# One fp32r product with high and low parts in place of a plain fp32 one, in the first attention of a two-block layer kernel

## What is computed

```
log_f = log_sigmoid(proj[..., COL_F:COL_RX] + b_forget)
c = cumsum(log_f, axis=1)
logits = einsum('bhqd,bhkd->bhqk', qb, kh) * scale
logits = logits + cb[..., :, None] - c[:, :, None, :]
probs = softmax(where(causal, logits, -inf))
```

## Time and profile before

| | before |
|---|---|
| median of 3 runs | 2224.82 us |
| lowest and highest | 2224.47, 2226.2 us |
| span of the profiled execution | 2226.0 us |
| its own total time | not given apart from the span; the slowest of the three runs has 2226.2 us |
| TensorE busy | 2156.0 us, 97% |
| DVE, ACT busy | 1316.3 us, 59%; 900.9 us, 40% |
| mean granted clock of TensorE | 0.997 |

### The profile page before, as it was taken

One profiled execution on the slowest core, in us unless ns is written; L12 is line 12 of the kernel. 1 busy time (PEld: TensorE's weight loads), 2 busy tenths in 40 slices (PEclk: granted clock), 3 DMA queues, 4 the chain that ended last, 5 costly groups with the idle time before them and its releaser, 6 DMA issues.

```text
span 2226.0 us, 31963 instructions
## 1 busy us (share of the span) xinstructions
PE 2156.0 (97%) x12035; PEld 1698.3 (76%) x12035; DVE 1316.3 (59%) x1788; ACT 900.9 (40%) x1188; POOL 15.7 (1%) x30
## 2 busy tenths in 40 slices
PE   9999999999889888999999999999999999999998
PEld 8887888655445444888888888888888888888886
DVE  7798566432222223766667665777777777764453
ACT  4564455411111112554435454554434343433342
POOL 1000000000000000000000000000000000000000
PEclk9999999999999999999999999999999999999999
DMA  7765466899999998556654555546666665666664
GB/s 252 214 204 152 133 186 207 319 421 420 420 422 421 421 421 336 178 173 218 211 173 162 162 157 185 169 152 190 189 188 188 188 188 188 188 209 191 196 191 131
DMA packets 283328, 518.39 MB, mean 233 GB/s; under 512 B 22048, under 2 KB 194128, under 8 KB 258512
## 3 DMA queue, kind: packets, MB, share of 16 engines
q1 hardware_dynamic: 280416, 505.50, 66.2%
q0 software_dynamic: 2800, 11.34, 1.5%
HBM read 514.63 MB, written 5.27 MB: 234 GB/s over the span
## 4 chain that ended last, share of the span: by engine, by line
PE 81%; DMA 11%; DVE 5%; ACT 2%; issue 1%; SPq 0%; DVEq 0%; ACTq 0%
PE acc L717 29%; PE acc L738 25%; PE acc L741 12%; DMA mw<-in_w_expert_up 7%; PE ps L1162 5%; PE acc L1242 3%; DMA mw<-in_w_expert_gate 2%; DVE wlo L1973 2%; DMA mw_late<-in_w_expert_up 2%; PE tp L826 1%; PE ps L894 1%; PE tp L1120 1%; PE tp L1110 0%; PE tp L909 0%; PE ps L841 0%
## 5 line engine op out<-in xcount | busy, mean ns | idle before, releaser
L1973 DVE TENSOR_TENSOR wlo<-raw,whi 128x1024 fp32r<-128x1024 f32 x572 | 675.9, 1220 | 209.5 <-ACT whi L1460 205.3
L738 PE MATMUL acc<-xhl,whi 128*128 128x512 f32 x2496 | 790.6, 398 | 1.6 <-DVE wlo L1973 0.7
L1460 ACT ACTIVATE whi<-raw 128x1024 fp32r<-128x1024 f32 x572 | 582.0, 1054 | 350.1 <-DMA raw<-in_w_down 132.1
L741 PEld LDWEIGHTS acc<-xhl,wlo 128*128 128x128 f32 x2496 | 468.9, 188 | 110.8
L741 PE MATMUL acc<-xhl,wlo 128*128 128x256 f32 x2496 | 490.8, 278 | 0.0
L738 PEld LDWEIGHTS acc<-xhl,whi 128*128 128x128 f32 x2496 | 381.4, 189 | 5.8 <-issue 3.0
L1162 PE MATMUL ps<-mw,xg_turn 128*64 128x256 f32 x1536 | 177.2, 384 | 29.3 <-DMA mw<-in_w_expert_gate 22.6
L1162 PEld LDWEIGHTS ps<-mw,xg_turn 128*64 128x64 f32 x1536 | 111.3, 138 | 98.7 <-issue 27.9
L717 PE MATMUL acc<-whi,xhl 128*128 128x512 f32 x480 | 155.9, 395 | 0.0
L717 PE MATMUL acc<-whi,ah 128*128 128x512 f32 x336 | 130.7, 389 | 0.0
L717 PE MATMUL acc<-wlo,ah 128*128 128x512 f32 x336 | 130.7, 389 | 0.0
(11 more groups left out here) (457 smaller groups left out, 2394.9 us busy)
## 6 DMA issues: line engine op xcount, KB each, us to landing
raw<-in_w_in SPq DMA_DIRECT2D x352, 256.0 KB, 3.0
raw<-in_w_up SPq DMA_DIRECT2D x352, 256.0 KB, 2.9
mw<-in_w_expert_up SPq DMA_DIRECT2D x52, 1024.0 KB, 16.5
mw<-in_w_expert_gate SPq DMA_DIRECT2D x50, 1024.0 KB, 17.4
mw<-in_w_expert_down SPq DMA_DIRECT2D x48, 1024.0 KB, 17.7
raw<-in_w_down SPq DMA_DIRECT2D x176, 256.0 KB, 3.3
raw<-in_w_out SPq DMA_DIRECT2D x128, 256.0 KB, 3.1
raw<-in_w_ple_gate SPq DMA_DIRECT2D x64, 256.0 KB, 3.3
```

The costliest lines, as they stand in the source:

```text
L738: pe.matmul(out(ct).rearrange("p (m n) -> p m n", m=2), wh[:, ct * P:ct * P + P], ahl[:, :, k, :], start=first, stop=False, skip_group_che ...
L741: mm = pe.matmul(out(ct)[:, S:2 * S], wl[:, ct * P:ct * P + P], ahl[:, 0, k, :], start=False, stop=last, skip_group_check=True)
L1460: act.activation(whi[:, m % RING, :], raw[:, m % RING, :], ACT.Copy).then_inc(hi_ready, 1)
L1973: dve.tensor_tensor(wlo[:, m % RING, :], raw[:, m % RING, :], whi[:, m % RING, :], ALU.subtract).then_inc(lo_ready, 1)
```

## The change

A second, fp32r, copy of negsel is made by ACT in two pieces: rows 0 to 31 of negsel go to partitions 0 to 31 and to 32 to 63 of negsel_r. DVE sets c_hl to zero, rounds c_cum to fp32r into partitions 0 to 7 of it, and writes the remainder to partitions 32 to 39. TensorE then multiplies the 64 partitions at once, so high and low part are subtracted in one fp32r product. The memset of c_cum is left out. The attention waits for ACT's copies (neg_ready) and no longer for late_in, for which ACT has waited by then. negsel_r lies where w_ing was, c_hl where diag is in other stages.

```diff
+        negsel_r = at("negsel_r", 77, [P, HEADS1, P], F32R)
+        c_hl = at("c_hl", 91.5, [P, S], F32R)
...
+        neg_ready = sem("neg_ready")
...
             pe.wait_ge(c_ready, 1)
-            pe.wait_ge(late_in, 48)
+            pe.wait_ge(neg_ready, 2)
 
             def minus_c(u, o, w):
 
-                return pe.matmul(o, negsel[:, u, :], c_cum[:, 0:w], start=False, stop=True, skip_group_check=True)
+                return pe.matmul(o, negsel_r[0:64, u, :], c_hl[0:64, 0:w], start=False, stop=True, skip_group_check=True)
...
             consume(4)
             root(3)
             squares(3)
+            for part in (0, 32):
+                act.activation(negsel_r[part:part + 32, :, :], negsel[0:32, :, :], ACT.Copy).then_inc(neg_ready, 1)
 
             consume(4)
             act.wait_ge(f_abs, 1)
...
-            own(dve.memset(c_cum[:, :], 0.0))
...
             dve.wait_ge(f_y, 1)
             own(dve.memset(z_1[:, :], 1.0))
+            own(dve.memset(c_hl[:, :].bitcast(F32), 0.0))
             log1p(z_y[:, :], z_z[:, :], z_q[:, :], z_s[:, :], z_n[:, :])
             own(dve.scalar_tensor_tensor(z_f[:, :], z_f[:, :], 0.0, z_n[:, :], ALU.min, ALU.subtract))
             mine()
-            dve.tensor_tensor_scan(c_cum[0:8, :], z_1[:, :], z_f[:, :], 0.0, ALU.mult, ALU.add).then_inc(c_ready, 1)
+            own(dve.tensor_tensor_scan(c_cum[0:8, :], z_1[:, :], z_f[:, :], 0.0, ALU.mult, ALU.add))
+            mine()
+            own(dve.tensor_copy(c_hl[0:8, :], c_cum[0:8, :]))
+            mine()
+            dve.tensor_tensor(c_hl[32:40, :], c_cum[0:8, :], c_hl[0:8, :], ALU.subtract).then_inc(c_ready, 1)
             dve.wait_ge(ms_root, 1)
             dve.reciprocal(inv[:, :], inv[:, :]).then_inc(inv_ready, 1)
```

## The result

The changed kernel takes 2236.43 us (median of 5, 2235.61 to 2239.2) against 2224.82 us (median of 5, 2224.47 to 2227.52): a ratio of 1.0049, 95% interval 1.0038 to 1.006, so 11.6 us more, where 5.65 were forecast. The time lies above the range. The profiled execution has a span of 2237.3 us (its own total is 2239.13) against 2226.0. A span is 1.8 to 1.9 us shorter than the total of its execution wherever both are given, so the profile before belongs to an execution of some 2227.9 us (an estimate from that difference), and both profiles are of slower executions of their kernels.

What follows compares the result with a forecast made beforehand. TensorE, 81% of the chain, was taken as the bound, with DVE's row setting the value projection stage. 2.97 - 0.25 + 1.53 + 1.4 = +5.65 us on 2224.82 gives 2230.5 us, range 2224.5 to 2232.5.

Steps and rivals of the forecast that it cites:

- TensorE's wait at 191: Value projection stage: TensorE waits 2.8 us at 191.41 for inv_lo, delayed by ACT's and DVE's added work.
- fall of the clock: After TensorE's stall near 191 us the granted clock drops to 1.2 GHz: +1.4 us (1.3 to 1.7).
- attention: Attention, 217 to 284 us: faster fp32r matmuls against tile-height changes, +1.53 us in sum over eight units (-3.9 to about +3.8).
- the fp32r rate: Attention's score matmuls: fp32r instead of plain fp32 saves 0.42 to 0.48 us a unit, 3.4 to 3.9 in eight.
- 27 borders: Attention: switches between 128-row and 64-row products, 0.2 us each, 12 on the path in units 0 to 2, 15 in the others.
- a unit led by TensorE: Attention units 0 to 2, TensorE without a gap: four borders count, +0.31 us each, 0.93 in three.
- a unit led by DVE: Attention units 3 to 7, DVE's chain the bound: three borders count, +0.12 us each, 0.6 in five.
- What is late at 284 us stays late.: From the attention's end to the kernel's end: the delay carries through unchanged, expert weight loads shifting too; nothing added.
- Rival 1: Value projection and attention: borders and stall, but no fall of the clock; +4.25, 2229.1 us; chance 0.28.
- Rival 2: Attention: borders cost nothing at L1022 in all eight units; -0.7, 2224.1 us (2225.5 with the clock's fall); chance 0.20.
- Rival 3: Attention: 128-column fp32r matmuls stay at 0.22 us; +1.3 more, 2231.8 us; chance 0.05.
- Rival 4: After 191.4 us: the stall is absorbed, replacing waits further on; +1.3, 2226 us; chance 0.03.

Runs made afterwards that it cites:

- 128 rows: Changed kernel with the product over 128 rows, ACT's copies later, DVE's c_hl operations moved into its q/k loop, four tiny fp32 products added in the first run-in: 2222.74 us, 0.9988.
- 64 rows: Changed kernel, still 64 rows, with ACT's copies later, DVE's c_hl operations moved into its q/k loop, four tiny fp32 products added in the first run-in: ratio 1.0008.
- the stall alone: Changed kernel with ACT's copies and DVE's operations kept, but TensorE multiplying plain fp32 negsel and c_cum, c_cum's memset back: 2231.79 us, ratio 1.0024.
- the best kernel without padding: Changed kernel with 128 rows, later ACT copies and moved DVE operations, without the four added fp32 products (16 instructions) in the first run-in: 2228.85 us, ratio 1.0011.
- the kernel before with padding: Kernel before the change plus four plain fp32 products of 4 columns (16 instructions) in the first run-in, nothing else: 2227.66 us, ratio 1.0009.

## Why the prediction was wrong

Point by point, forecast and trace:

| step | forecast, us | shown, us |
|---|---|---|
| ACT's copies | +1.94 | 2.14 (first split 169.30 to 171.44) |
| DVE's operations | +1.03 | 1.13 (16.17 less 15.04) |
| TensorE's wait at 191 | 2.8 | 2.89 |
| fall of the clock | +1.4 | with the wait +4.31 at 217 us, so 1.3 to 1.4 |
| removed memset | -0.25 | -0.28 at the first matmul |
| attention | +1.53 | +1.42 (to the output projection), +1.54 (first to last product) |
| of it the fp32r rate | -3.4 to -3.9 | -3.4 (128 rows: -0.85 at 217 us, -4.28 at 284) |
| of it 27 borders | +5.4 | +4.85 (64 rows: -0.93, +0.49) |
| a unit led by TensorE | +0.31 | +0.29 to the end of the fill's first two matmuls, +0.30 from unit to unit |
| a unit led by DVE | +0.12 | +0.10 |
| to the end | 0 | +6.1 |

**The step that failed is "What is late at 284 us stays late."** The forecast put the term from there to the end at nothing, and the runs showed 6.1 us. The sentence held for DMA and semaphores, which it argued from: +5.15 us at 284 are +5.22 at 850.89. What it left out is that the change also makes TensorE's program shorter, and that a program is itself fetched. The row that would have asked for it stood in the trace of the kernel before: a wait of 3.9 us on "issue", right behind a branch, can be an engine that waits for its own instructions. None of the four rivals had it. With 6.1 us more the forecast would have been 2236.6 us, against 2236.43; that they agree to 0.2 us is partly luck, since the sum up to 284 us was 0.5 too high and the kernel's own runs lie up to 3.6 us apart.

The forecast also took the profile before for an execution as long as the slowest of the three (2226.0 beside 2226.2), and so set a span beside totals; it used only the difference, so nothing in its sum changes. Its clock term is 1.7 less 0.4, which is 1.3 and not 1.4, inside its own bounds.

The sum up to 284 us, +5.65, came out at +5.15. A part of the difference is at the start: TensorE was 0.58 us ahead at 165 us and not 0.25. But this place scatters: the twelve other kernels lie between -0.02 and -1.57 us there, the unchanged program part included, as the clock rises sooner or later behind the first matmuls (the first 32 matmul records take 6.58 us in some executions and 5.31 in another).

Rival 1 (no fall of the clock) did not happen; in all seven kernels that stood still for 2.5 us or more there (2.53 to 3.26) the clock fell, for 3.4 or 6.8 us, and in none of the others. The forecast had one length of the fall; it has two, and the longer costs 1.5 us more (the stall alone: 5.8 instead of 4.3). Its reason, that the stall is longer than the two waits it knew, isn't borne out as a rule: behind the same wait of 2.06 us at 420 us of the kernel before, the clock fell in nine traces and not in the five others, and of the six in which TensorE stood still for 2.3 to 2.7 us at 613 it fell in one. So the fall was forecast rightly, and in part by luck. Rival 2, borders that cost nothing, needs weight loads that start ahead of their matmuls; with 64 rows none of the sixteen does, with 128 rows all do. The Trainium skill, page "TensorE: Matmul & The Clock Gate", section "Part 2: What happens when you issue a matmul", says that rows don't matter to a load's time, and the traces agree: 0.18 us with 64 rows, 0.19 with 128. It also says that loads are pulled ahead of running matmuls if the row groups don't conflict or the load goes to the background buffer. Here that was seen between tiles of one height and not at a border between 64 and 128 rows; which of the two conditions failed there, no run shows. So the forecast's reading, that these loads wait, held: a border costs time because the load starts late and nothing hides it, not because the load is longer. Rival 3, 128 columns at 0.22 us, is refuted: with 128 rows the matmul of 128 columns is followed within 0.15 us (216.54 to 216.69 above), in all units of the three kernels with 128 rows. Rival 4 was tested by the stall alone and didn't hold.

For the fetch, the Trainium skill, page "Runtime: NRT & Kernel Launch", section "Instruction fetch mechanics", says that prefetch is sequential and that a taken branch to a target outside the window stops the engine until the target's page is there. The trace agrees with that: the wait is 3.85 us in the kernel before and 3.46 to 3.74 in the others but one, where it is 2.53. There the clock had fallen at 827 us and TensorE came later to the wait, while the packet and the matmul behind it kept their distance of 2.63 us. That a second wait can follow, and when, is what the runs here add. That a block ends where the matmuls stop is worked out from the counts 1, 5 and 9; the traces show when packets of instructions came and how large they are, one more in each of the kernels with two waits (78) than in each with one (77), but not which instructions are in them.

**The measured parts, put together.** The stall alone gives a ratio of 1.0024, the attention with its borders 1.0008, the second wait 1.0023 (the best kernel without padding, 1.0011, against 0.9988 with it), in all 1.0055 where the change has 1.0049 (1.0038 to 1.006). The parts are not clean: the kernel of the attention has in it the gain of the faster product and of the start, and the cost of the padding, if any, and each ratio is uncertain by 0.001. The second wait itself is worth 5.3 to 6.0 us by the traces across the branch (833 to 859 us), and by medians 3.9 (taken out of the changed kernel), 5.1 (out of the 128-row kernel) and 7.1 (put into the kernel before).

## What to carry to other kernels

Where an engine's program has a branch that is taken, look for waits on "issue" behind it, and count how many of its instructions a change adds or removes ahead of it; a few idle instructions ahead of the branch can move the landing to a better place, or a few less to a worse one, and the timeline tells which. Keep the operands of neighbouring matmuls at one tile height, with zero rows if need be: here that was worth 4.8 us in 16 products. And what an engine computes for a later use belongs behind the work that another engine is waiting for: the copies and the split of c cost 4.3 us in front of it, with the fall of the clock, and nothing behind (the 128-row kernel comes to 217 us with no delay).

## What the runs showed of the hardware

- Behind the branch TensorE stood still for 3.5 to 3.9 us in thirteen of fourteen traces, and where the next block was waited for, it landed 5.4 to 5.7 us after the first, whatever ran meanwhile. An estimate from that: with more than some 5.5 us of work between the landing and the end of its block (some 40 of these matmuls, by 8.57 us for 64 in the kernel before) no second wait would be seen. The six kernels with one wait fit it, but no run tried where the limit lies.
- The wait behind the branch brought the lower clock in all fourteen traces. With one wait the stretch was 3.4 us long, with two 10.2.
- A border between products of 128 and of 64 rows costs 0.18 us, by 4.85 us over the 27 on the path, where the second attention's rows gave 0.2.
- Stretches at the lower clock came and went elsewhere between executions of kernels that differ in nothing there (the kernel before with padding gained 1.7 us on the kernel before at 420 us, because its clock did not fall). They make single spans uncertain by 2 to 3 us; the ratios come from medians.
- The length of a wait alone didn't decide whether the clock fell: after 2.53 to 3.26 us at 191 us it fell in seven traces of seven, after 2.06 at 420 us in nine of fourteen, after 2.3 to 2.7 at 613 us in one of six.
